# Two transformer blocks on one core: the dense matmuls as one plain float32 matmul each in place of three over rounded parts

## The chip, the cores and the metric

The kernel runs on one core of one Trainium2 chip. The metric is the device time of that core in microseconds, from the first to the last instruction of one launch. Lower is better.

## What is computed

256 tokens of width 1024, in float32, go through two blocks. The reference, cut to what matters:

```python
# first block (c gives shift, scale and gate of both halves: ada = silu(c) @ w_ada + b_ada)
h = modulate(rmsnorm(x, g), sh_m, sc_m)
proj = h @ w_in                       # 1024 -> cq, ckv, k_rope, fq, fk, fv, f_logit, g_mla, g_fox
q  = rmsnorm(cq) @ w_uq;  kv = rmsnorm(ckv) @ w_ukv
y  = sigmoid(g_mla) * (attention(q, k, v) @ w_o_mla) + sigmoid(g_fox) * (attention(fq, fk, fv, log_cum) @ w_o_fox)
x  = x + g_m * (y @ w_out)
h  = modulate(rmsnorm(x, g), sh_f, sc_f)
u  = causal_conv3(h @ w_up)           # 1024 -> 5632
x  = x + g_f * ((silu(gate) * val) @ w_down)
x  = rmsnorm(x)
# second block
proj = rms_norm(x) @ w_in_2           # xc, b_gate, c_gate, q, k, v
h  = x + concat(short_conv(xc, b_gate, c_gate), diff_attention(q, k, v)) @ w_out_2
hn = rms_norm(h)                      # 4 groups of 8 experts, the best 2 of the best group
out = h + sum over the experts e of (silu(hn @ w_gate[e]) * (hn @ w_up[e]) * comb[:, e]) @ w_down[e]
```

## The kernel before

It is one program written by hand for the five engines, ordered by semaphores. There is no scheduler: the order on each engine is the order of the code.

**The dense part.** All dense weights (w_in, w_uq, w_ukv, w_o_mla, w_o_fox, w_out, w_up, w_down, w_in_2, w_out_2, and w_ada for the vector c) are a list of `items` that SyncE (SP) loads one after the other into a ring of three slots of SBUF (line 407). An item of w_in, w_up or w_in_2 is 1024 x 512 float32, 2 MB; `up0` to `up10` are the items of w_up, `dn0` to `dn5` those of w_down, and `q2`, `k2`, `v2`, `xc`, `cg`, `bg`, `w2o_attn` and `w2o_conv` those of the second block. An item is worked off in chunks, of 128 x 1024 weights as a rule.

**The three passes.** A dense product is made of float32r operands, which TensorE reads in reduced precision. Each operand is split in a high part, rounded to float32r, and a low part, the rest. For each chunk, `split` on ScalarE (ACT, line 590) copies the raw weights into `wh` (one of four buffers), and `split` on VectorE (DVE, line 1451) subtracts it from the raw weights into `wl`. The activations are held in two parts as well: `hH` and `hL` (the normed input, by feature), `aH` and `aL` (attention output, latents, the activated FFN), `hnH` and `hnL` (the normed tokens for the experts). Where an activation is produced, ACT writes the high part and DVE then the low one (lines 1477, 1593, 1677, 1723, 1768, 1846, 1963, 1981). `chunk` on TensorE (PE) waits for `chunk_low` and issues for every 128 x 128 block of weights

```python
o_ = ps[:, b0 + m // 2, 256 * (m % 2):256 * (m % 2) + 256]
mm(o_, h[:, cs], xh[:, k, :], st and m % 2 == 0, False)
mm(o_, h[:, cs], xl[:, k, :], False, False)
ins = mm(o_, l[:, cs], xh[:, k, :], False, sp_)
```

where the weights are stationary and the 256 tokens move. For `cq`, `ckv`, `fv`, `uq`, `ukv`, `q2`, `k2` and `v2` it is the other way round (`by_token`): 128 tokens are stationary, and 288 to 512 columns of weights move.

**The order of the dense part** is: projections of the first block; its attention in 16 steps, between which `chunk` puts the gate items g1 to g3; output projections; up and down (items up0 to up5, dn0 to dn2, up6 to up10, dn3 to dn5); norms; q2, k2, v2, xc; the second attention in 8 steps with cg and bg between; the output projection; the router.

**The experts.** All 32 experts are worked off in 8 turns of four, in two pairs (r = 0 and r = 1), for the tokens that chose them (64 places for each expert). `gather` picks the tokens by a product of `hnH` and `hnL` with a matrix of zeros and ones, `pick`, which is float32r too. After it come gate, up, four transposes of the product (line 1410), down, and the product with `putT` that adds the rows to `y_acc`. Gate, up, down and putT are plain float32 matmuls. The gather for the next turn is issued at the end of a turn, and a last one, whose result nobody reads, after the last turn. The 201 MB of expert weights go through eight places of 2 MB: slots 0 to 2 (the ring), 3, 4 and 5 (`work`), 6, and 7 in two halves (`slot7a`, `slot7b`, the latter in `wb`). Slots 6 and 3 and slot7a share memory with `wl`, `wh` and `hL`, so their first loads wait for the last dense chunk. In the loop SP waits for `expert_used` before it loads a place again (lines 475 to 488).

Activations (`Silu`, `Exp`, `Square`) are on ACT, everything else that is elementwise on DVE, and the power of -0.5 of the norms on GpSimd (POOL).

## Time and profile before

| | |
|---|---|
| median of 3 runs | 1144.72 us (1140.96 to 1156.25) |
| profiled execution, its span | 1145.6 us |
| dense part, to the first expert matmul | 643.95 us |
| experts, to the end | 501.7 us |
| busy: PE, its weight loads, DVE, ACT | 90%, 60%, 39%, 34% |
| mean granted TensorE clock | 0.967 |

The profiled execution has no time of its own beside its span; the span stands 0.9 us above the median of the runs. A matmul's busy time overlaps that of the next one, so the time that a stream of matmuls takes is read from the distance of their starts, or from how many there are in a stretch without a gap.

### The profile page before, as it was taken

The numbers are of one execution on the slowest core, as the hardware profiler recorded it, in microseconds if no ns is written. First come the engines' busy times: TensorE is split into PE (matmuls) and PEld (weight loads), VectorE is DVE, ScalarE is ACT, GpSimd is POOL, SyncE is SP. The second block draws the span as 40 slices with busy tenths as digits, with TensorE's granted clock in tenths as the row PEclk, the third lists the DMA queues.
The fourth block names the chain that finished last, engine by engine and source line by source line (L and its number), as shares of the span: only waits on it lengthen the run. The fifth ranks groups of instructions, "written<-read, shape, count | busy, mean of one in ns | idle before, by whom it ended". The sixth has DMA issues, their size and how long they took to land.

```text
span 1145.6 us, 15408 instructions
## 1 busy us (share of the span) xinstructions
PE 1034.9 (90%) x6222; PEld 681.7 (60%) x6222; DVE 444.5 (39%) x829; ACT 388.7 (34%) x675; POOL 23.6 (2%) x50
## 2 busy tenths in 40 slices
PE   3799899999899999979889799999989899798888
PEld 1497767888799999958788434343424224242323
DVE  1543455657578467566664310101111100110111
ACT  0343444554566456445544212030302103020302
POOL 1000000000000000012010000000000000000000
PEclk9799999999899999989889899999989999999999
DMA  9663943284355563625627699999999999999996
GB/s 322 258 220 123 364 184 147 75 285 156 114 181 192 177 199 132 221 89 205 221 88 257 222 379 375 348 387 387 387 387 387 387 387 387 387 387 387 387 387 225
DMA packets 156329, 309.06 MB, mean 270 GB/s; under 512 B 6738, under 2 KB 32376, under 8 KB 153208
## 3 DMA queue, kind: packets, MB, share of 16 engines
q1 hardware_dynamic: 153496, 307.17, 74.0%
q10 hardware_dynamic: 2784, 1.21, 0.4%
q8 instruction: 35, 0.57, 0.2%
q14 instruction: 14, 0.11, 0.0%
HBM read 307.31 MB, written 1.05 MB: 269 GB/s over the span
## 4 chain that ended last, share of the span: by engine, by line
PE 27%; SPq 16%; DMA 5%; DVE 2%; issue 1%; ACT 1%; ACTq 0%; DVEq 0%
PE ps L952 26%; SPq L414 8%; SPq L451 6%; DMA work<-w_exp_down 3%; DMA wb<-w_exp_gate 3%; SPq L418 2%; DVE wc L2080 1%; PE ps L1410 1%; ACT wc L941 0%; PE ps L1332 0%; DVE wb L1896 0%; PE ps L1263 0%; PE ps L1384 0%; DVE wa L1887 0%; DVE wl L1451 0%
## 5 line engine op out<-in xcount | busy, mean ns | idle before, releaser
L1451 DVE TENSOR_TENSOR wl<-ring,wh 128x1024 fp32r<-128x1024 f32 (+4 forms) x156 | 184.1, 1191 | 119.7 <-ACT wh L590 119.3
L590 ACT ACTIVATE wh<-ring 128x1024 fp32r<-128x1024 f32 (+4 forms) x156 | 159.6, 1031 | 149.7 <-PE ps L952 121.8
L952 PE MATMUL ps<-hH,wh 128*128 128x256 f32 x704 | 203.2, 289 | 5.9 <-DVE hL L1477 1.9
L952 PE MATMUL ps<-hH,wl 128*128 128x256 f32 x704 | 199.7, 284 | 0.0
L952 PE MATMUL ps<-hL,wh 128*128 128x256 f32 x704 | 199.7, 284 | 0.0
L952 PE MATMUL ps<-slot,xT 128*64 128x512 f32 x384 | 174.2, 610 | 16.8 <-DMA wb<-w_exp_gate 16.8
L952 PE MATMUL ps<-ring,xT 128*64 128x512 f32 x512 | 168.5, 594 | 1.0 <-DMA slot<-w_exp_up 1.0
L952 PEld LDWEIGHTS ps<-hH,wh 128*128 128x128 f32 x704 | 135.7, 193 | 12.1 <-issue 7.3
L952 PEld LDWEIGHTS ps<-hL,wh 128*128 128x128 f32 x704 | 135.0, 192 | 0.2
L952 PEld LDWEIGHTS ps<-hH,wl 128*128 128x128 f32 x704 | 135.0, 192 | 0.0
L952 PE MATMUL ps<-work,wc 128*64 128x512 f32 x512 | 115.1, 597 | 17.4 <-ACT wc L941 11.0
L952 PEld LDWEIGHTS ps<-ring,xT 128*64 128x64 f32 x512 | 52.5, 137 | 108.4 <-issue 104.8
L2080 DVE TENSOR_TENSOR wc<-wc,ps 128x512 f32<-128x512 f32 x16 | 11.0, 687 | 271.4 <-PE ps L952 271.4
L2093 DVE TENSOR_TENSOR wb<-wb,ps 128x512 f32<-128x512 f32 x64 | 44.0, 687 | 160.3 <-PE ps L952 160.3
L952 PE MATMUL ps<-aH,wh 128*128 128x256 f32 x304 | 86.9, 286 | 2.2 <-DVE aL L1677 1.7
L952 PEld LDWEIGHTS ps<-slot,xT 128*64 128x64 f32 x384 | 53.0, 140 | 59.6 <-issue 38.7
L952 PEld LDWEIGHTS ps<-work,wc 128*64 128x64 f32 x512 | 34.6, 137 | 87.7 <-issue 58.9
L952 PE MATMUL ps<-aL,wh 128*128 128x256 f32 x304 | 86.1, 283 | 0.0
L952 PE MATMUL ps<-aH,wl 128*128 128x256 f32 x304 | 86.1, 283 | 0.0
L952 PE MATMUL ps<-wa 128*128 128x512 f32 (+2 forms) x160 | 71.7, 570 | 0.9 <-ACT work L710 0.9
L952 PEld LDWEIGHTS ps<-aH,wh 128*128 128x128 f32 x304 | 58.4, 192 | 3.0 <-DVE aL L1677 1.9
L952 PEld LDWEIGHTS ps<-aL,wh 128*128 128x128 f32 x304 | 58.1, 191 | 0.0
(310 smaller groups left out, 1240.7 us busy)
## 6 DMA issues: line engine op xcount, KB each, us to landing
work<-w_exp_down SPq DMA_DIRECT2D x64, 1024.0 KB, 14.3
ring<-w_exp_up SPq DMA_DIRECT2D x32, 1024.0 KB, 14.2
ring<-w_exp_gate SPq DMA_DIRECT2D x32, 1024.0 KB, 14.1
slot<-w_exp_up SPq DMA_DIRECT2D x32, 1024.0 KB, 14.2
ring<-w_ada SPq DMA_DIRECT2D x12, 2048.0 KB, 9.1
ring<-w_in SPq DMA_DIRECT2D x12, 2048.0 KB, 8.5
ring<-w_up SPq DMA_DIRECT2D x22, 1024.0 KB, 7.3
slot<-w_exp_gate SPq DMA_DIRECT2D x8, 2048.0 KB, 17.0
```

What stands on the lines that cost most here:

```text
L414: sp.dma_start(slot(i)[:, k0 * width:(k0 + kn) * width].rearrange("p (k n) -> p k n", k=kn), src[:, k0:k0 + kn, :])\
L418: sp.dma_start(dst.rearrange("p (k n) -> p k n", k=4), expert(w_gate, e)[:, k0:k0 + 4, :])\
L451: sp.dma_start(to, expert(w_downx, e + j)[:, :, cs]).then_inc(S(f"downs_half{half}"), 16)
L590: nc.scalar.activation(wh[:, c % CHUNKS, 0:n], src, ACT.Copy).then_inc(S("chunk_high"), 1)
L952: return nc.tensor.matmul(o_, l, r, start=start, stop=stop, skip_group_check=True)
L1410: ins = nc.tensor.transpose(ps[:, 2, f * P:f * P + P], eact[:, f * P:f * P + P], ident[:])
L1451: V.tensor_tensor(wl[:, c % CHUNKS, 0:n], src, wh[:, c % CHUNKS, 0:n].bitcast(F32), ALU.subtract)\
L2080: V.tensor_tensor(eact, sg, ps[:, 1, :], ALU.mult).then_inc(S("e_act"), 1)
L2093: V.tensor_tensor(v, v, ps[:, 6 + i % 2, :], ALU.add).then_inc(S("y_sum"), 1)
```

## The change

Each dense product is one plain float32 matmul: `chunk` reads the raw weights from the ring slot and the activations from one tensor (`hT`, `aT`, `hn_tok`), with a third of the calls. Both `split` functions go, with every step that writes a low part; what wrote the high part now writes the operand (where DVE made a float32 tensor first, it writes the operand itself). `gather` has one product where there were two, and `pick` is float32. The dense ring has five slots, 0, 1, 2, 3 and 6, and an item is waited for by PE at its first chunk; SP waits for `chunk_used` (PE is done with the item) where it waited for `chunk_low` (the item is split). slot7a is memory of its own, and its first load stands ahead of the others.

```diff
 SLOT = 8 * 520
-RING1 = 3
-CHUNK = 2 * 520
-CHUNKS = 4
+RING_SLOTS = (0, 1, 2, 3, 6)
...
+        ring = sb("ring", [P, len(RING_SLOTS), SLOT])
         work = sb("work", [P, 2 * SLOT])
-
-        with nc.sbuf_tensor("wl", [P, CHUNKS, CHUNK], F32R) as wl:
-            pass
-        slot6 = sb("slot6", [P, SLOT])
-        with nc.sbuf_tensor("wh", [P, CHUNKS, CHUNK], F32R) as wh:
-            pass
-        slot3 = sb("slot3", [P, SLOT])
-        with nc.sbuf_tensor("hL", [P, KD, SEQ], F32R) as hL:
-            pass
         slot7a = sb("slot7a", [P, KD * SEQ])
-        hH = sb("hH", [P, KD, SEQ], F32R)
-        aH = sb("aH", [P, 12, SEQ], F32R)
-        aL = sb("aL", [P, 12, SEQ], F32R)
+        hT = sb("hT", [P, KD, SEQ])
...
         for i, it in enumerate(items):
-            it["slot"] = i % RING1
+            it["slot"] = RING_SLOTS[i % len(RING_SLOTS)]
...
-                if i == RING1:
+                if i == 3:
                     load_rows()
-                if i >= RING1:
-                    before = items[i - RING1]
+                if i >= len(RING_SLOTS):
+                    before = items[i - len(RING_SLOTS)]
                     if before["chunks"]:
-                        sp.wait_ge(S("chunk_low"), before["c1"])
+                        sp.wait_ge(S("chunk_used"), before["c1"])
                     else:
...
-            for i in sorted(last, key=lambda i: last[i]["c1"]):
-                sp.wait_ge(S("chunk_low"), last[i]["c1"])
+            final = {it["slot"]: it["c1"] for it in items}
+            in_order = sorted(final, key=lambda i: final[i])
+            for i in in_order:
+                if i == in_order[-2]:
+                    sp.wait_ge(S("att_logits"), 2 * HEADS + 2 * N_HEADS2)
+                    load_half7(slot7b, 3, 4)
+                sp.wait_ge(S("chunk_used"), final[i])
                 if i < 2:
                     for half in range(2):
                         load_gate_half(i, i, half)
+                elif i < 4:
+                    load_up(i - 2, i - 2)
                 else:
-                    load_up(0, 0)
-            sp.wait_ge(S("att_logits"), 2 * HEADS + 2 * N_HEADS2)
-            load_half7(slot7b, 3, 4)
-            sp.wait_ge(S("chunk_used"), n_chunk)
-            load_up(1, 1)
-            load(6, expert(w_gate, 2), 0, KD, D_EXP, "slot6_loaded")
-            load_half7(slot7a[:], 3, 0)
+                    load(6, expert(w_gate, 2), 0, KD, D_EXP, "slot6_loaded")
...
 
-            def split(name, a=0, b=None):
-
-                it = IT[name]
-                for ci in range(a, len(it["chunks"]) if b is None else b):
-                    c = it["c0"] + ci
-                    if ci == 0:
-                        act.wait_ge(S(f"slot{it['slot']}_loaded"), it["loaded"])
-                    if c >= CHUNKS:
-                        act.wait_ge(S("chunk_used"), c - CHUNKS + 1)
-                    src, n = raw_chunk(it, ci)
-                    nc.scalar.activation(wh[:, c % CHUNKS, 0:n], src, ACT.Copy).then_inc(S("chunk_high"), 1)
...
-                        ins = nc.scalar.activation(hH[:, k, :], n_t[:, k, :], ACT.Identity, bias=shift[:, k:k + 1])
-                    ins.then_inc(S("norm_high"), 1)
+                    nc.scalar.activation(hT[:, k, :], n_t[:, k, :], ACT.Identity, bias=shift[:, k:k + 1])\
+                        .then_inc(S("norm_in"), 1)
 
...
@@ -951,47 +833,37 @@
             def mm(o_, l, r, start, stop):
                 return nc.tensor.matmul(o_, l, r, start=start, stop=stop, skip_group_check=True)
 
-            def chunk(name, ci, xh, xl, by_token, banks=None, first=True, last=True, ready=None):
+            def chunk(name, ci, x, by_token, banks=None, first=True, final=True, ready=None):
 
                 it = IT[name]
                 n = it["n"]
                 b0 = it["acc"] if banks is None else banks
                 main = n if n > 520 else min(n, 512)
                 k0, kn = it["chunks"][ci]
-                c = it["c0"] + ci
-                pe.wait_ge(S("chunk_low"), c + 1)
-                for kk in range(kn):
-                    k = k0 + kk
+                if ci == 0:
+                    pe.wait_ge(S(f"slot{it['slot']}_loaded"), it["loaded"])
+                w = slot_view(it)
+                for k in range(k0, k0 + kn):
                     if ready is not None:
                         pe.wait_ge(S(ready[0]), ready[1][k])
-                    st, sp_ = first and k == 0, last and k == it["kn"] - 1
-                    h = wh[:, c % CHUNKS, kk * n:(kk + 1) * n]
-                    l = wl[:, c % CHUNKS, kk * n:(kk + 1) * n]
+                    st, sp_ = first and k == 0, final and k == it["kn"] - 1
                     if by_token:
                         for tt in range(TT):
                             ts = slice(tt * P, tt * P + P)
-                            o_ = ps[:, b0 + tt, 0:main]
-                            mm(o_, xh[:, k, ts], h[:, 0:main], st, False)
-                            mm(o_, xl[:, k, ts], h[:, 0:main], False, False)
-                            ins = mm(o_, xh[:, k, ts], l[:, 0:main], False, sp_)
+                            ins = mm(ps[:, b0 + tt, 0:main], x[:, k, ts], w[:, k, 0:main], st, sp_)
                             if n > main:
-                                o_ = ps[:, 4, tt * (n - main):(tt + 1) * (n - main)]
-                                mm(o_, xh[:, k, ts], h[:, main:n], st and tt == 0, False)
-                                mm(o_, xl[:, k, ts], h[:, main:n], False, False)
-                                ins = mm(o_, xh[:, k, ts], l[:, main:n], False, sp_)
+                                ins = mm(ps[:, 4, tt * (n - main):(tt + 1) * (n - main)], x[:, k, ts], w[:, k, main:n],
+                                         st and tt == 0, sp_)
                     else:
                         for m in range(n // P):
-                            cs = slice(m * P, m * P + P)
-                            o_ = ps[:, b0 + m // 2, 256 * (m % 2):256 * (m % 2) + 256]
-                            mm(o_, h[:, cs], xh[:, k, :], st and m % 2 == 0, False)
-                            mm(o_, h[:, cs], xl[:, k, :], False, False)
-                            ins = mm(o_, l[:, cs], xh[:, k, :], False, sp_)
+                            ins = mm(ps[:, b0 + m // 2, 256 * (m % 2):256 * (m % 2) + 256], w[:, k, m * P:m * P + P], x[:, k, :],
+                                     st and m % 2 == 0, sp_)
                 ins.then_inc(S("chunk_used"), 1)
 
...
+                        pe.wait_ge(S("hn_high"), i + 2)
                     for kk in range(2):
                         k = 2 * i + kk
                         o_ = ps[:, 6 + i % 2, 256 * kk:256 * kk + 256]
                         for tt in range(TT):
-                            mm(o_, hnH[:, tt, k * P:k * P + P], pick[:, tt, :], kk == 0 and tt == 0, False)
-                            ins = mm(o_, hnL[:, tt, k * P:k * P + P], pick[:, tt, :], False, tt == TT - 1)
+                            ins = mm(o_, hn_tok[:, tt, k * P:k * P + P], pick[:, tt, :], kk == 0 and tt == 0, tt == TT - 1)
                     ins.then_inc(S("gathered"), 1)
...
 
-            def split(name, a=0, b=None):
-
-                it = IT[name]
-                for ci in range(a, len(it["chunks"]) if b is None else b):
-                    c = it["c0"] + ci
-                    dve.wait_ge(S("chunk_high"), c + 1)
-                    src, n = raw_chunk(it, ci)
-                    V.tensor_tensor(wl[:, c % CHUNKS, 0:n], src, wh[:, c % CHUNKS, 0:n].bitcast(F32), ALU.subtract)\
-                        .then_inc(S("chunk_low"), 1)
...
                 for k in range(KD):
-                    V.scalar_tensor_tensor(out=n_t[:, k, :], in0=xT[:, k, :], scalar=scale[:, k:k + 1], in1=bc,
-                                           op0=ALU.mult, op1=ALU.mult).then_inc(S("norm_t"), 1)
-                    if k >= 2:
-                        low(k - 2)
-                low(KD - 2)
-                low(KD - 1)
+                    out_, sem = (n_t, "norm_t") if shifted else (hT, "norm_in")
+                    V.scalar_tensor_tensor(out=out_[:, k, :], in0=xT[:, k, :], scalar=scale[:, k:k + 1], in1=bc,
+                                           op0=ALU.mult, op1=ALU.mult).then_inc(S(sem), 1)
 
...
-            split("dn5")
-            split("q2", 0, 2)
             done("dn5")
             for m in range(KD):
                 residual(m, ps[:, 4 + m // 2, 256 * (m % 2):256 * (m % 2) + 256], adaT[:, G_F + m:G_F + m + 1], "xT_ready")
 
 
             cols = norm_mean(2, 3, 2)
-            split("q2", 2, 3)
             dve.wait_ge(S("norm_rstd"), 3)```

**PE, in one of the first block's attention steps** (ident and wc at line 1145: the turn of a head's probabilities; wa and nFT: the scores of the head two steps on). Before:

```order
L952 MATMUL ps<-hH,wh 128x256
L952 MATMUL ps<-hL,wh 128x256
L952 MATMUL ps<-hH,wl 128x256
L1145 MATMUL ps<-ident,wc 128x128 x3
L952 MATMUL ps<-wa 128x128
L952 MATMUL ps<-nFT,ident 128x128
```

The first three rows stand eight times in a row. After, the same step:

```order
L834 MATMUL ps<-hT,ring 128x256 x8
L1017 MATMUL ps<-ident,wc 128x128 x3
L834 MATMUL ps<-wc,wa 64x256
L834 MATMUL ps<-wc,wa 64x128
L834 MATMUL ps<-wa 128x128
L834 MATMUL ps<-nFT,ident 128x128
```

The 24 calls of a chunk are 8, and nothing else on PE is moved.

**DVE, at the second norm of the first block** (L1482 writes `n_t`, which ACT turns into hH; L1477 writes hL). Before:

```order
L1464 COPY wc<-ps 1x256
L1458 TENSOR_SCALAR ms<-ps 128x2
L1451 TENSOR_TENSOR wl<-ring,wh 128x1024
L1482 SCALAR_TENSOR_TENSOR wb<-xT,scale_f,ps 128x256 x3
L1477 SCALAR_TENSOR_TENSOR hL<-wb,adaT,hH 128x256
```

After:

```order
L1325 COPY wc<-ps 1x256
L1319 TENSOR_SCALAR ms<-ps 128x2
L1335 SCALAR_TENSOR_TENSOR wb<-xT,scale_f,ps 128x256 x8
L1561 SCALAR_TENSOR_TENSOR work<-ps,colT,work 128x255 x4
L1561 SCALAR_TENSOR_TENSOR work<-ps,colT,work 128x254 x4
```

The first part that PE can use came behind three steps of DVE, one of ACT and a fourth of DVE; now it comes behind one of DVE and one of ACT.

**SP, at the end of the dense part.** Before:

```order
L451 DMA work<-w_exp_down 128x4x512 [waits k2_turned]
L451 DMA work<-w_exp_down 128x4x512 x3
L414 DMA ring<-w_exp_up 128x4x512 [waits chunk_low]
L414 DMA ring<-w_exp_up 128x4x512
L414 DMA ring<-w_exp_gate 128x4x512 [waits chunk_low]
L414 DMA ring<-w_exp_gate 128x4x512
L414 DMA ring<-w_exp_gate 128x4x512 [waits chunk_low]
L414 DMA ring<-w_exp_gate 128x4x512
L418 DMA wb<-w_exp_gate 128x4x512 [waits att_logits]
L414 DMA slot<-w_exp_up 128x4x512 [waits chunk_used]
L414 DMA slot<-w_exp_up 128x4x512
L414 DMA slot<-w_exp_gate 128x8x512
```

After:

```order
L391 DMA slot7a<-w_exp_gate 128x4x512
L424 DMA work<-w_exp_down 128x4x512 [waits k2_turned]
L424 DMA work<-w_exp_down 128x4x512 x3
L387 DMA ring<-w_exp_gate 128x4x512 [waits chunk_used]
L387 DMA ring<-w_exp_gate 128x4x512
L387 DMA ring<-w_exp_up 128x4x512 [waits chunk_used]
L387 DMA ring<-w_exp_up 128x4x512
L387 DMA ring<-w_exp_up 128x4x512 [waits chunk_used]
L387 DMA ring<-w_exp_up 128x4x512
L391 DMA wb<-w_exp_gate 128x4x512 [waits att_logits]
L387 DMA ring<-w_exp_gate 128x8x512 [waits chunk_used]
L387 DMA ring<-w_exp_gate 128x4x512 [waits chunk_used]
```

Five places (3, 6 and 7a among them) no longer wait together for the last chunk of all: only one of the ring's slots does.

## Rows read from the trace of the kernel before

**Rows 1.** The page: busy time and count by engine; granted clock and GB/s in 40 slices.
```profile
PE 1034.9 (90%) x6222; PEld 681.7 (60%) x6222; DVE 444.5 (39%) x829; ACT 388.7 (34%) x675; POOL 23.6 (2%) x50
...
PEclk9799999999899999989889899999989999999999
...
GB/s 322 258 220 123 364 184 147 75 285 156 114 181 192 177 199 132 221 89 205 221 88 257 222 379 375 348 387 387 387 387 387 387 387 387 387 387 387 387 387 225
```

**Rows 2.** Busy time (and records) by engine in three stretches, with clock and GB/s.
```profile
300.00:330.00 30.00, 30.00 (x256) 30.00 (x255) 21.70 (x31) 17.91 (x24) 0.00 (x0) 1.00 0.44 141
503.00:530.00 27.00, 27.00 (x118) 21.95 (x117) 18.97 (x25) 11.83 (x13) 3.81 (x1) 1.00 0.42 142
698.00:702.00 4.00, 4.00 (x33) 3.82 (x33) 0.59 (x1) 2.48 (x6) 0.00 (x0) 1.00 1.05 387
```

**Rows 3.** PE's groups by shape: stationary size, moving form, records | busy, mean ns | idle before.
```profile
L952 PE MATMUL ps<-hH,wh 128*128 128x256 f32 x704 | 203.2, 289 | 5.9 <-DVE hL L1477 1.9 <-ACT wb L682 1.4 <-DVE wl L1451 1.1
...
L952 PE MATMUL ps<-aH,wh 128*128 128x256 f32 x304 | 86.9, 286 | 2.2 <-DVE aL L1677 1.7 <-issue 0.6
...
L952 PE MATMUL ps<-wa 128*128 128x512 f32 x128 | 62.2, 618 | 0.0
L952 PE MATMUL ps<-hH,aH 128*128 128x256 f32 x144 | 38.6, 304 | 1.5 <-DVE hH L2031 1.5
...
L952 PE MATMUL ps<-wh,hH 128*128 128x512 f32 x64 | 27.4, 428 | 1.8 <-DVE hL L1475 1.8
```

**Rows 4.** PE's timeline: start, length, engine, line, matmul, count; five stretches.
```profile
713.68 0.59 PE L952 MATMUL ps<-ring,xT 128*64 128x512 f32 x1
...
714.11 0.59 PE L952 MATMUL ps<-ring,xT 128*64 128x512 f32 x1
...
284.70 3.61 PE L952 MATMUL ps<-wb,tri_ones 128*1 128x256 f32 x16
...
192.28 0.92 PE L952 MATMUL ps<-work 96*128 96x128 f32 x4
...
152.03 0.70 PE L952 MATMUL ps<-wa 64*128 64x256 f32 x2
...
152.66 0.52 PE L952 MATMUL ps<-nFT,ident 8*128 8x256 f32 x1
```

**Rows 5.** What PE waited for: us in total, times, longest; whole span.
```profile
PE ps L952 <- DMA wb<-w_exp_gate: 16.8, 5, 3.4
...
PE ps L952 <- DVE hL L1477: 4.2, 2, 2.3
...
PE ps L1263 <- DVE wa L1841: 3.2, 2, 2.1
PE ps L952 <- DVE wl L1451: 2.7, 2, 1.5
PE ps L952 <- DVE wb L1865: 2.6, 1, 2.6
PE ps L952 <- DVE hL L1475: 1.8, 1, 1.8
```

**Rows 6.** PE's timeline: the transposes of four pairs of experts.
```profile
658.69 0.66 PE L1410 MATMUL ps<-ident,wc 128*128 128x128 f32 x4 [0.79 <-DVE wc L2080]
...
717.22 0.66 PE L1410 MATMUL ps<-ident,wc 128*128 128x128 f32 x4 [0.79 <-DVE wc L2080]
...
964.45 0.66 PE L1410 MATMUL ps<-ident,wc 128*128 128x128 f32 x4 [0.79 <-DVE wc L2080]
...
1028.88 0.66 PE L1410 MATMUL ps<-ident,wc 128*128 128x128 f32 x4 [0.79 <-DVE wc L2080]
```

**Rows 7.** SP's queue, a stretch of the loop's start.
```profile
702.41 2.65 SPq L451 DMA_DIRECT2D work<-w_exp_down  x1
716.64 0.39 SPq L414 DMA_DIRECT2D ring<-w_exp_up  x1
```

**Rows 8.** PE's timeline: the first record of the last gather.
```profile
1140.20 0.39 PE L952 MATMUL ps<-hH,aH 128*128 128x256 f32 x1
```

More of the change, by code:

```diff
@@ L9 @@
 F32 = mybir.dt.float32
-F32R = mybir.dt.float32r
 I32 = mybir.dt.int32
@@ L162, in slot @@
         def slot(i):
-            if i < RING1:
-                return ring[:, i, :]
-            return {3: slot3[:], 4: work[:, 0:SLOT], 5: work[:, SLOT:2 * SLOT], 6: slot6[:]}[i]
+            if i in RING_SLOTS:
+                return ring[:, RING_SLOTS.index(i), :]
+            return {4: work[:, 0:SLOT], 5: work[:, SLOT:2 * SLOT]}[i]
         rows = wc[:, 0:3 * P].rearrange("p (i n) -> p i n", i=3)
@@ L451, in load_downs @@
                         sp.dma_start(to, expert(w_downx, e + j)[:, :, cs]).then_inc(S(f"downs_half{half}"), 16)
+            load_half7(slot7a[:], 3, 0)
             sp.wait_ge(S("k2_turned"), 2)
             load_downs(0)
-            last = {it["slot"]: it for it in items}
-            for i in sorted(last, key=lambda i: last[i]["c1"]):
-                sp.wait_ge(S("chunk_low"), last[i]["c1"])
+            final = {it["slot"]: it["c1"] for it in items}
[5 more added lines that the diff above has]
+                sp.wait_ge(S("chunk_used"), final[i])
                 if i < 2:
@@ L752, in _ @@
                     nc.scalar.activation(v, v, ACT.Sigmoid).then_inc(S("sig_ready"), 1)
-            split("wo0", 0, 2)
-            for m in range(KD):
-                if m == 4:
-                    split("wo0", 2)
-                act.wait_ge(S("y_ready"), m // 2 + 1)
-                nc.scalar.activation(hH[:, m, :], yF[:, m, :], ACT.Copy).then_inc(S("y_high"), 1)
-            split("wo1")
-            split("up0", 0, 3)
             norm_squares(1)
-            split("up0", 3)
-            norm_high(1, adaT[:, SH_F:SH_F + KD])
+            norm_shift(1, adaT[:, SH_F:SH_F + KD])
             def conv_first(j):
@@ L1063, in _ @@
             ada_turn(0)
-            linear("cq", hH, hL, True, ready=("norm_in", [IN_BASE[0] + k + 1 for k in range(KD)]))
-            linear("ckv", hH, hL, True)
+            linear("cq", hT, True, ready=("norm_in", [IN_BASE[0] + k + 1 for k in range(KD)]))
+            linear("ckv", hT, True)
             pe.wait_ge(S("lat_copied"), 2)
-            linear("fq", hH, hL, False)
+            linear("fq", hT, False)
             pe.wait_ge(S("ada_row"), 1)
@@ L1108, in _ @@
                     ada_turn(1)
-                chunk("g0", ci, hH, hL, False)
+                chunk("g0", ci, hT, False)
             pe.wait_ge(S("rope_done"), 1)
@@ L1174, in _ @@
                         pe.wait_ge(S("gate_out"), 2 * (i // 4) + 2)
-                    chunk(f"g{1 + i // 4}", i % 4, hH, hL, False)
+                    chunk(f"g{1 + i // 4}", i % 4, hT, False)
                 turn(a)
@@ L1287, in _ @@
                 if st < 4:
-                    chunk("cg", st, hH, hL, False)
+                    chunk("cg", st, hT, False)
                 else:
@@ L1291, in _ @@
                         pe.wait_ge(S("cg_out"), 2)
-                    chunk("bg", st - 4, hH, hL, False)
+                    chunk("bg", st - 4, hT, False)
                 if st % 2:
@@ L1302, in _ @@
             pe.wait_ge(S("cy_ready"), 2)
-            o_in = ("mix_low", [1, 2, 3, 4])
-            chunk("w2o_attn", 0, aH[:, 4:8], aL[:, 4:8], False, 0, True, False, o_in)
+            o_in = ("mix_high", [1, 2, 3, 4])
+            chunk("w2o_attn", 0, aT[:, 4:8], False, 0, True, False, o_in)
             pe.wait_ge(S("cv_sq"), 1)
@@ L1323, in _ @@
             ins.then_inc(S("cv_bc"), 1)
[L1324 to L1325 removed]
+            chunk("w2o_attn", 3, aT[:, 4:8], False, 0, True, False, o_in)
+            linear("w2o_conv", aT, False, 0, False, True, ("mixF", [1, 2, 3, 4]))
             for i in range(4):
@@ L1393, in _ @@
                             elif part == 0:
-                                pe.wait_ge(S("slot6_loaded"), turn * 16 + 16)
+                                pe.wait_ge(S("slot6_loaded"), turn * 16 + (base_loaded[6] + 16))
                                 pe.wait_ge(S("slot7_loaded"), turn * 32 + 32)
@@ L2013, in _ @@
             V.tensor_tensor(gtmp, gl, wide(gmax, GROUPS), ALU.subtract).then_inc(S("g_shift"), 1)
-            for i in range(2):
-                low_tokens(i)
             dve.wait_ge(S("places"), 1)
@@ L2045, in _ @@
             pick_tokens(0, 0)
-            for i in range(2, 4):
-                low_tokens(i)
             link(V.tensor_scalar(npass[0:1, 1:2], npass_f[0:1, 0:1], float(CAP - 1), None, ALU.add))
```

291 lines of the change are left out of this document (54 added, 237 removed).

## The prediction

> **What bounds the kernel now.** I first read the page [rows 1]: PE is busy for 90% of the span, DVE and ACT for 39% and 34%, and the memory moves 387 GB/s without a dip in the last third, far below that before. So there are two parts with different limits, and each is read for itself.
>
> In the dense part (643.95 us) the question is whether PE or the splitting on ACT and DVE sets the pace. The windows answer it [rows 2]: from 300 to 330 us there are 256 records of 256 columns in 30.00 us without idle time, 117 ns for each, 118 with a chunk's own edges. From 503 to 530 us records of 512 columns come at 27.00/118 = 229 ns. ACT and DVE are idle for a third of that time and more. A column thus costs PE some 0.45 ns whatever the others do, and the splits are ahead. What PE waited for in this part [rows 5] is 1 to 4 us at single places, most of it behind a step that writes a low part. The dense part is bound by PE's stream of columns.
>
> In the experts' part (501.7 us) PE is near the limit too. The transposes of turn after turn start 717.22 - 658.69 = 58.53 us apart at first, and 1028.88 - 964.45 = 64.43 us late in the loop [rows 6]. A turn loads 25.2 MB, which takes 65.0 us at 387 GB/s [rows 1]. So PE sets the first turns and the memory the later ones; PE's wait for slot7b, 16.8 us in five times of up to 3.4 [rows 5], is that limit seen from PE.
>
> **What a plain float32 matmul costs.** The groups by shape [rows 3] count 128 records for the products with putT, of which the program has 64 (8 turns, 2 pairs, 4 products): a plain matmul is two records, one for each half of its stationary operand. The timeline [rows 4] gives the length of one: gate and up records of 512 columns on the same columns of the array start 714.11 - 713.68 = 0.43 us apart, and the 16 records of 256 columns of a norm's sum take 3.61 us to the end of the last, whose own length is about 0.38: 15 distances of 0.215 us. Four records of 128, 128, 256 and 256 columns on 96 rows end 0.92 us after they start, with no more than the two streams in it. So a record costs 0.215 us at 256 columns and 0.43 at 512, twice a float32r record, and the matmul has two of them: 0.43 and 0.86 us. Three float32r records are 3 x 0.118 = 0.354 and 3 x 0.230 = 0.690 us. **The change takes a third of the calls away and makes each product dearer on the engine that bounds the part.** The trace has no plain matmul with 128 x 128 weights and 256 moving columns; 0.215 a record is the row nearest in columns. From below it is the stream alone, 0.427/2 = 0.213; from above it is the scores on half the rows, where two records take 152.66 - 152.03 = 0.63 us, 0.32 each, since the weights' load is not hidden there [rows 4]. I take 0.216, as the products with putT and the 96-row scores have full or nearly full weights and show no such gap.
>
> The Trainium skill (FP8 and Floating Point Precision, "TensorE Precision Notes") has true FP32 at "4 passes through PE array". At four times a 256-column stream the matmul is an estimate of 0.43 us; the 0.215 us of a record with two records to a matmul agree.
>
> **The change part by part.**
> 1. *Blocks with 256 moving tokens.* 704 + 304 = 1008 [rows 3], each 0.432 - 0.354 = 0.078 us dearer: **+78.6 us**. Nothing hides it: PE has no idle time in those stretches.
> 2. *Token-major products with 512 columns.* 64 [rows 3] and 8 of ukv: 72 x (0.86 - 0.69) = **+12.0 us**.
> 3. *Token-major products with 384, 288 and 8 columns* (28, 16 and 16 in the code). In proportion to columns the first two add about 0.12 and 0.09 us each; the last, two short records for three, gives some back. I take **+3 us**, bounds 0 and +6.
> 4. *Gather.* A gather is 32 float32r records at 4.00/33 = 0.121 us [rows 2], 3.9 us; it becomes 32 records of 0.216, 6.9 us: +3.1 us each time. The first lies ahead of the experts: **+3.1 us**. Those of turns 1 to 7 lie in a PE turn of 58.5 us, which becomes 61.6, still under the memory's 65.0: hidden, as long as the memory stays the limit, and the cover is 3.4 us a turn. Ahead of that limit one is not hidden: SP's loads of the next ups wait until 716.64 us for PE, when the queue has run dry behind the loads of 702.41 [rows 7]. They come 3.1 us later, and all the stream after them: **+3.1 us**. The last gather starts at 1140.20 [rows 8], behind everything, and ends the program: **+2.8 us**.
> 5. *Splits and low parts.* 156 splits each on ACT and DVE go. They hide behind PE's stream today and bring nothing there. They bring something where PE waited for them [rows 5]: the two waits for `wl` go whole (2.7); the three at a norm's end shorten from four steps of DVE and one of ACT to one or two steps in all (3.3 of 6.0); the attention's ends, where DVE had splits before the step that PE waited for, give about 3.5 of 5.8; and half a microsecond comes from the low part of the last head. **-10 us**, bounds -5 and -15 (all of these rows).
> 6. *The ring of five.* PE waited for no dense weights, so deeper prefetch brings nothing. At the end of the dense part the expert places are filled earlier, but they were full before too: PE waits for none of them in the first turns. **0**, bounds 0 and -3. The loads at the start stand in the same order up to the rows of small vectors; two more come right behind these and could hold up nothing that PE awaits but those rows: 0 to +1.
>
> Short stretches at 1.2 GHz (the lower digits of the clock, [rows 1]) follow the waits at the norms. They are counted in time, not in matmuls, and stay as they are.
>
> Sum: 78.6 + 12.0 + 3 + 3.1 + 3.1 + 2.8 - 10 = **+92.6 us**. From the span that is 1145.6 + 92.6 = 1238.2; from the median of the runs, 0.9 lower, **1237 us**.
>
> **The rivals.**
> - *The plain matmul streams once (faster).* If one record of 256 columns at 0.215 did a whole product, the 1008 blocks would save 0.139 us each, 140 us, and with the token-major ones and the waits the time would be near 980. The point from which this side decides is 0.354/2 = 0.177 us a record (0.172 with what the waits give back). For it: the code calls one matmul. Against it: two records for every plain call, and 0.215 each. 2%.
> - *The splits are the limit, and PE only looks busy.* Then taking them away gains more than the matmuls cost. Its place would be the up and down items; ACT at 17.91 and DVE at 21.70 of 30 us, with PE without a gap [rows 2], speak against it. No change at best, 1145. 2%.
> - *The weights' load comes into the open.* At 0.32 us a record [rows 4] the blocks cost 0.64 instead of 0.432, 210 us more: about 1450. The 96-row scores speak against it. 3%. The Trainium skill says it as a rule (TensorE: Matmul & The Clock Gate, "What overlaps and what doesn't"): a weight load overlaps a running matmul only when the row groups differ. By that rule the dense stream, always on the same 128 rows, would pay each load. The 117 ns of the float32r stream, on the same rows throughout, do not agree with it.
> - *The gathers are not hidden.* If PE stays the limit in all turns, because the loads wait for PE more often than I read, seven more gathers count: up to +18 us, 1255. PE's own turn of 61.6 us is near 65.0, which speaks for some of it. 10%.
> - *More of the waits go than I took*, and the experts' loads gain: 1222 to 1230. 10%.
>
> **How the numbers follow.** The forecast holds with 73%: 1237, itself good to some 9 us (4 ns on a record's price alone are 8 us over 2016 records). Bounds of the small terms and the last two rivals widen it to 1218 to 1258. Faster by over 2% (the first rival) 2%, within 2% 2%, slower by over 2% 96%; 2% is about what a measurement of this kernel can tell from no change.
>
> **What would show it.** In the changed kernel, groups with 1408 + 608 records for the blocks and 288 for the gather; some 139 records in a window of 30 us of the up items, against 256; no idle PE there. The first expert matmul at 644 + 87 = 731 us. The transposes of turns 0 and 1 some 61.6 us apart and those of the late turns 65, with PE's wait for slot7b near nothing. DVE and ACT some 200 us less busy each. Wrong would I be if records of the blocks came closer than 0.21 us or farther apart than 0.23, or if the late turns took more than 66 us.

## The result and the profile after

The changed kernel takes 1230.08 us (median of four runs, 1229.28 to 1230.53) against 1147.17 (four runs, 1140.96 to 1156.25): 1.0712 times as long, 95% interval 1.0663 to 1.0762. The forecast was 1237, range 1218 to 1258. The profiled executions span 1228.0 us and, before, 1145.6.

The page of the changed kernel, busy time and count by engine, clock and GB/s in 40 slices:

```profile
PE 1140.7 (93%) x5082; PEld 696.7 (57%) x5082; DVE 239.5 (20%) x611; ACT 221.7 (18%) x488; POOL 19.1 (2%) x50
...
PEclk9899979999999999999999989999999999999999
...
GB/s 329 153 356 105 361 136 104 69 231 214 111 164 137 138 160 149 137 192 82 171 274 104 137 125 387 311 379 387 387 387 387 387 387 387 387 387 387 387 387 204
```

PE has 1140 records fewer than in [rows 1] and 106 us more to do. DVE and ACT have lost 205 and 167 us of work, nearly all of which lay beside PE's stream.

PE's groups by shape:

```profile
L834 PE MATMUL ps<-hT,ring 128*128 128x256 f32 x1408 | 312.0, 382 | 2.3 <-ACT hT L582 1.3 <-DVE wb L1689 1.0
...
L834 PE MATMUL ps<-aT,ring 128*128 128x256 f32 x608 | 134.6, 383 | 1.3 <-issue 0.8 <-ACT aT L672 0.5
...
L834 PE MATMUL ps<-hT,aT 128*128 128x256 f32 x288 | 67.2, 393 | 1.5 <-DVE hT L1773 1.5
```

1408 + 608 records for 1008 blocks: two to each product, as forecast, where [rows 3] had three. Here is a window of the up items, with busy time (and records) of PE, PEld, DVE, ACT and POOL, then granted clock, DMA share, GB/s:

```profile
330.00:360.00 30.00, 30.00 (x140) 26.41 (x140) 7.99 (x18) 6.41 (x11) 0.00 (x0) 1.00 0.41 140
```

30.00/140 = 0.214 us a record, without a gap, against 256 records in [rows 2]. A stretch with nothing else in it prices the block: the 96 blocks of dn0 to dn2 take 41.44 us (401.49 to 442.93), 0.432 each; in the kernel before they take 34.12 (364.68 to 398.80), 0.355.

PE's timeline: the first expert matmul, the transposes of the first two turns and of the last three, the last gather:

```profile
721.09 2.37 PE L834 MATMUL ps<-ring,xT 128*64 128x512 f32 x10
...
735.84 0.65 PE L1281 MATMUL ps<-ident,wc 128*128 128x128 f32 x4 [0.79 <-DVE wc L1820]
...
797.22 0.66 PE L1281 MATMUL ps<-ident,wc 128*128 128x128 f32 x4 [0.79 <-DVE wc L1820]
...
1046.17 0.66 PE L1281 MATMUL ps<-ident,wc 128*128 128x128 f32 x4 [0.79 <-DVE wc L1820]
1111.22 0.66 PE L1281 MATMUL ps<-ident,wc 128*128 128x128 f32 x4 [0.79 <-DVE wc L1820]
1176.28 0.66 PE L1281 MATMUL ps<-ident,wc 128*128 128x128 f32 x4 [0.79 <-DVE wc L1820]
...
1219.71 7.17 PE L834 MATMUL ps<-hT,aT 128*128 128x256 f32 x32
```

The dense part ends at 721.09, 77.1 us later than before (86.7 were forecast). The experts take 1228.0 - 721.09 = 506.9 us, 5.3 more (5.9 were forecast). Turns start 61.38 us apart at first and 65.05 late, as forecast from [rows 6]. From span to span the change costs 82.4 us where the sum in the prediction was 92.6, and the miss of some 10 us lies in the dense part.

What PE waited for: us in total, times, longest:

```profile
PE ps L834 <- DMA work<-w_exp_down: 6.2, 4, 2.1
PE ps L834 <- DMA wb<-w_exp_gate: 5.5, 4, 1.5
...
PE ps L834 <- POOL rstd L524: 3.1, 3, 1.0
PE ps L834 <- ACT hT L582: 2.9, 2, 1.6
...
PE ps L834 <- ACT wb L733: 1.0, 1, 1.0
...
PE ps L834 <- DVE r L1588: 0.8, 1, 0.8
...
PE ps L834 <- DVE hT L1335: 0.7, 1, 0.7
```

The waits for `hL` (4.2 and 1.8 in [rows 5]) have become 2.9 and 0.7, those for `wl` are gone, 2.6 before the second attention is 1.0. The wait for slot7b fell from 16.8 to 5.5, and gave back nothing by itself: the memory was the limit there.

### The profile page after: what moved, and what is told of

Its sections match the earlier page's. It is cut to its first block, busy times and chain, and to the rows that moved or that the text cites. A ratio compares the mean times of both kernels' runs of the same rounds, so it can differ in the third digit from the quotient of the medians.

```text
span 1228.0 us, 12648 instructions
## 1 busy us (share of the span) xinstructions
PE 1140.7 (93%) x5082; PEld 696.7 (57%) x5082; DVE 239.5 (20%) x611; ACT 221.7 (18%) x488; POOL 19.1 (2%) x50
## 3 DMA queue, kind: packets, MB, share of 16 engines
HBM read 307.31 MB, written 1.05 MB: 251 GB/s over the span
## 4 chain that ended last, share of the span: by engine, by line
PE 73%; SPq 21%; DVE 2%; DMA 2%; issue 1%; ACT 1%; POOL 0%; ACTq 0%; DVEq 0%
PE ps L834 71%; SPq L387 10%; SPq L424 7%; SPq L391 3%; SPq L349 1%; DMA work<-w_exp_down 1%; DMA wc<-lambda_k 0%; DVE wc L1820 0%; PE ps L1017 0%; PE ps L1281 0%; ACT wc L823 0%; PE ps L993 0%; PE ps L1204 0%; POOL rstd L524 0%; PE ps L1255 0%
## 5 line engine op out<-in xcount | busy, mean ns | idle before, releaser
L834 PE MATMUL ps<-hT,ring 128*128 128x256 f32 x1408 | 312.0, 382 | 2.3 <-ACT hT L582 1.3
L834 PEld LDWEIGHTS ps<-hT,ring 128*128 128x128 f32 x1408 | 267.7, 191 | 44.2 <-issue 6.6
L834 PE MATMUL ps<-ring,xT 128*64 128x512 f32 x896 | 224.1, 594 | 6.8 <-DMA wb<-w_exp_gate 5.5
L834 PEld LDWEIGHTS ps<-ring,xT 128*64 128x64 f32 x896 | 70.9, 137 | 152.8 <-issue 139.2
L834 PE MATMUL ps<-aT,ring 128*128 128x256 f32 x608 | 134.6, 383 | 1.3 <-issue 0.8
L834 PE MATMUL ps<-work,wc 128*64 128x512 f32 x512 | 114.3, 596 | 17.2 <-ACT wc L823 11.0
L834 PEld LDWEIGHTS ps<-aT,ring 128*128 128x128 f32 x608 | 116.2, 192 | 17.8 <-issue 1.2
L834 PEld LDWEIGHTS ps<-work,wc 128*64 128x64 f32 x512 | 35.0, 137 | 86.2 <-issue 61.3
L834 PE MATMUL ps<-ring,hT 128*128 128x512 f32 (+2 forms) x224 | 80.4, 519 | 2.3 <-ACT hT L582 1.6
L834 PE MATMUL ps<-wa 128*128 128x512 f32 (+2 forms) x160 | 72.8, 578 | 0.9 <-ACT work L653 0.9
L834 PE MATMUL ps<-hT,aT 128*128 128x256 f32 x288 | 67.2, 393 | 1.5 <-DVE hT L1773 1.5
L1820 DVE TENSOR_TENSOR wc<-wc,ps 128x512 f32<-128x512 f32 x16 | 11.0, 688 | 279.6 <-PE ps L834 279.6
L1561 DVE SCALAR_TENSOR_TENSOR work<-ps,colT,work 128x255 f32<-128x255 f32 (+1 forms) x88 | 36.3, 475 | 146.7 <-ACT work L701 146.3
L834 PEld LDWEIGHTS ps<-ring,hT 128*128 128x128 f32 x224 | 41.4, 197 | 41.2 <-issue 35.2
L834 PEld LDWEIGHTS ps<-hT,aT 128*128 128x128 f32 x288 | 55.8, 196 | 15.4 <-DVE wb L1833 6.0
L834 PEld LDWEIGHTS ps<-wa 128*128 128x128 f32 (+1 forms) x160 | 25.5, 191 | 47.4 <-issue 25.6
L826 ACT ACTIVATE wa<-ps 128x512 f32<-128x512 f32 x32 | 19.1, 598 | 112.6 <-PE ps L834 112.6
L834 PE MATMUL ps<-ring,cact 128*1 128x512 f32 x192 | 26.4, 682 | 10.9 <-ACT cact L586 10.9
```

The costliest lines, as they stand in the source:

```text
L826: nc.scalar.activation(eout[:, 512 * hf:512 * hf + 512], ps[:, 3 + hf, :], ACT.Copy)\
L834: return nc.tensor.matmul(o_, l, r, start=start, stop=stop, skip_group_check=True)
L1561: ins = V.scalar_tensor_tensor(out=v, in0=src, scalar=colT[:, ROW[row] + tile:ROW[row] + tile + 1], in1=v, op0=ALU.mult, op1=ALU.add)
L1820: V.tensor_tensor(eact, sg, ps[:, 1, :], ALU.mult).then_inc(S("e_act"), 1)
```

## The experiments

Three questions: are the forecast's terms right one by one, where did 10 us more relief come from, and is there a version that beats both kernels. The kernel before was timed again with each group: medians of 1153.38 (first four kernels), 1149.28 (next four) and 1148.32 (last three). It scatters by 15 us, the changed kernel by 1; so plain versions are best compared with 1230.08, and the stages of the profiled runs with each other. The changed kernel was not timed again, while the median of the one before moved by 5 us from group to group; a difference of plain versions counts only where the spans of the profiled runs show it too.

Two sums over the dense part are used below. One is all that PE waited: 61.6 us before, 49.4 in the changed kernel. The other is what slow clock costs. At 1.2 GHz plain records of 256 columns start 0.427 us apart where they start 0.216 apart at 2.4 GHz (splits_beside, 323 to 327 us), float32r records 0.213 where they start 0.118 apart (the kernel before, 294 to 301 us). So of PE's busy time in the stretches with a granted clock of 0.5, half is lost, or 45% for float32r records. By this estimate it is 23.2 us before and 18.5 in the changed kernel.

**1. plain_with_splits.** `chunk` of the kernel before reads the raw slot:

```diff
-    mm(o_, h[:, cs], xh[:, k, :], st and m % 2 == 0, False)
-    mm(o_, h[:, cs], xl[:, k, :], False, False)
-    ins = mm(o_, l[:, cs], xh[:, k, :], False, sp_)
+    ins = mm(ps[:, b0 + m // 2, 256 * (m % 2):256 * (m % 2) + 256], h[:, m * P:m * P + P],
+             xh[:, k, :].bitcast(F32), st and m % 2 == 0, sp_)
 # h is slot_view(it)[:, k, :]; the same for by_token. SP:
-    sp.wait_ge(S("chunk_low"), before["c1"])
+    sp.wait_ge(S("chunk_used"), before["c1"])
```

> The kernel before with one thing changed: each dense product is one plain float32 matmul that reads the raw weights in the ring and the high part of the activations (the low parts of both are made and waited for, but not used, so the sum lacks them). Every split, every wait for a low part, the ring of three and the gather with two products stay. Theory (the forecast's +78.6, +12 and +3 for the matmuls are right, and what was missing, some 10 us more relief than taken, comes from the splits' absence): 1147 + 94 = 1241 us, good to 4. Rival (the plain matmuls cost less than the forecast says, and the splits' absence gave the 10 us that were forecast): 1231.

Measured: 1266.55 us (1259.31 to 1267.8), ratio 1.0971 (1.0914 to 1.1028). Above both, so it decides between neither. The experiment had a second change in it that I had priced at nothing: a slot is held until PE is done with it. Runs 2, 3 and 4 take the two apart.

**2. ring_of_three.** The changed kernel with the dense items in three slots:

```diff
+DENSE = (0, 1, 2)
-    it["slot"] = RING_SLOTS[i % len(RING_SLOTS)]
+    it["slot"] = DENSE[i % len(DENSE)]
 # and the experts' first loads in the order of the kernel before
```

> The changed kernel with the dense items in slots 0, 1 and 2 alone; slots 3 and 6 stay empty until the loads of the experts, which stand in the order of the kernel before. Theory (PE waits for no dense weights, deeper prefetch brings nothing): 1230 to 1231. Rival (the ring of five is where the unforeseen 10 us come from): 1236 to 1240, with waits of PE for the ring's loads in the dense part.

Measured: 1240.66 us (1239.10 to 1243.45), 10.6 more than the changed kernel. Its first expert matmul starts at 732.72, 11.6 later, and PE has a wait that the changed kernel hasn't:

```profile
PE ps L835 <- DMA ring<-w_in: 8.0, 2, 5.5
```

5.5 us before ckv and 2.5 before g0. PE waits 8.3 us more in the dense part, and slow clock costs 2.8 more, 11.1 of the 11.6 together. The theory of the ring falls for the changed kernel, and the rival (1236 to 1240) holds: with three slots it takes 10.6 us more.

**3. late_release.** The kernel before with that wait of SP alone:

```diff
-    sp.wait_ge(S("chunk_low"), before["c1"])
+    sp.wait_ge(S("chunk_used"), before["c1"])
 # the same ahead of the experts' first loads
```

> The kernel before, with SP waiting until PE is done with a slot's last chunk (as the changed kernel does) before it loads the slot again, where it waited for the split alone. Nothing else is changed. Theory (a ring of three that is held longer lets PE run out of weights; that is why ring_of_three lost 10 us and why the ring of five is worth something in the changed kernel): slower than before by 8 to 20 us, with waits of PE for low parts of weights that hang on a load. Rival (the three slots suffice in the kernel before in either case): no change.

Measured: 1182.93 us (1179.08 to 1184.78), ratio 1.0294 (1.0238 to 1.0351): some 34 us, all in the dense part, and more than the bound that I gave. PE's waits:

```profile
PE ps L952 <- DVE wl L1451: 12.8, 5, 7.2
...
PE ps L1145 <- DVE wc L1672: 7.0, 2, 5.2
```

The first was 2.7 [rows 5]. A slot freed when its last chunk is split is free up to four chunks before PE is done with it; in the kernel before, this is what made three slots enough. All waits in the dense part grow by 23.6 us, from 61.6 to 85.2. The rest is slow clock, which costs 33.8 us where it cost 23.2; PE runs at 1.2 GHz through most of these 16 us:

```profile
172.00:188.00 16.00, 16.00 (x63) 9.62 (x62) 6.32 (x19) 3.48 (x11) 0.00 (x0) 0.57 0.40 133
```

**4. splits_beside.** The clean form of run 1: five slots, and the splits' results in small scratch places.

```diff
+    wl = sb("wl", [P, CHUNK], BF16)
+    wh = sb("wh", [P, 2, CHUNK], BF16)
-    nc.scalar.activation(wh[:, c % CHUNKS, 0:n], src, ACT.Copy)
+    nc.scalar.activation(wh[:, c % 2, 0:n], src, ACT.Copy)
-    V.tensor_tensor(wl[:, c % CHUNKS, 0:n], src, wh[:, c % CHUNKS, 0:n].bitcast(F32), ALU.subtract)
+    V.tensor_tensor(wl[:, 0:n], src, src, ALU.subtract)
```

> The changed kernel's matmuls, gather and ring of five slots, with all the work of the splits put back beside them: ACT copies every chunk and DVE subtracts on every chunk, at the places in the program and with the waits of the kernel before, and the low parts of the activations are made and waited for. Their results go to small scratch places (bfloat16, the same number of elements) and are not used, so the sum lacks the low parts. Theory (the ring of three that was held until PE was done spoiled the run plain_with_splits, and the splits' absence gave all of the dense part's relief, 19.6 us): 1250 us, good to 4. Rival (of the relief only the norms' 5 us and some 5 at the attention are the splits', the rest comes from the plain stream itself, behind which more can hide): 1240. Rival (the late slots were innocent, splits beside plain matmuls cost what plain_with_splits shows): 1262 and more.

Measured: 1245.13 us (1243.68 to 1245.98), 15.0 above the changed kernel, half way between the theory (1250, good to 4) and the first rival (1240); the first expert matmul at 735.33, 14.2 later. The up items show that the splits themselves cost nothing beside the stream, as many records in 30 us as without them:

```profile
335.00:365.00 30.00, 30.00 (x141) 26.41 (x140) 19.39 (x29) 16.94 (x22) 0.00 (x0) 1.00 0.41 140
```

What they cost is waits at a stage's edge, and these are the rows of before again, but for `wl` (2.7 there):

```profile
PE ps L956 <- POOL rstd L552: 4.9, 3, 2.0
...
PE ps L956 <- DVE hL L1474: 4.2, 2, 2.3
...
PE ps L956 <- DVE wb L1862: 2.6, 1, 2.6
PE ps L956 <- DVE wl L1448: 2.1, 2, 1.5
PE ps L956 <- DVE hL L1472: 1.8, 1, 1.8
PE ps L956 <- DVE r L1803: 1.8, 1, 1.8
PE ps L956 <- DVE aL L1674: 1.7, 1, 1.7
```

Against the changed kernel's rows (3.1; 2.9; 1.0; none; 0.7; 0.8; 0.5) that is 19.1 - 9.0 = 10.1 us of waits, of 10.8 in all. Slow clock makes up most of the rest of the 14.2: it costs 22.0 us in this run and 18.5 in the changed kernel, 3.5 more.

**5. norm_chains.** The changed kernel with the old chains in the three norms alone:

```diff
+    def low(k):
+        dve.wait_ge(S("norm_high"), IN_BASE[n] + k + 1)
+        V.tensor_tensor(junk[:, k, :], xT[:, k, :], hT[:, k, :], ALU.subtract).then_inc(S("norm_in"), 1)
```

> The changed kernel with the steps put back that stood in the three norms' chains before: DVE writes a stand-in for the low part behind each normed piece, two pieces late, and PE waits for it; a DVE step as long as a split stands at the three places where a split stood in the second and third norm. Nothing else is changed. Theory (the unforeseen relief is shorter waits at the norms and the stretches at 1.2 GHz behind them, which come back with the waits): PE's waits there grow by some 5 us, a granted clock of 0.5 is seen again behind the second norm, the third or both, and the time is 1238, 8 us more. First rival (waits alone, the clock does not follow them): 1235. Second rival (the relief lies elsewhere, as at the attention's ends): 1230 to 1232.

Measured: 1235.99 us (1234.96 to 1236.95), 5.9 more, the first rival. The first expert matmul starts 4.9 us later, and PE's waits there grew by 5.0: 5.8 for `junk`, 4.9 for `rstd`, 1.8 for `r`, against 3.6, 3.1 and 0.8. (A wait for a small load at another place is 1.6 us shorter.) Slow clock did come back at the norms, as the theory had it (at 315 to 318 us, and at 554 to 564 where the changed kernel has 556 to 559), but it went elsewhere: in the dense part it costs 18.8 us against 18.5.

**6. two_product_gather.** The changed kernel with the old gather:

```diff
-    ins = mm(o_, hn_tok[:, tt, k * P:k * P + P], pick[:, tt, :], kk == 0 and tt == 0, tt == TT - 1)
+    mm(o_, hnH[:, tt, k * P:k * P + P], pick[:, tt, :], kk == 0 and tt == 0, False)
+    ins = mm(o_, hnL[:, tt, k * P:k * P + P], pick[:, tt, :], False, tt == TT - 1)
```

> The changed kernel with the gather as it was before: high and low part of the normed tokens, two float32r products with 256 columns, and DVE's four steps that write the low part. Theory (terms of part 4: first gather 3.1, the stall of SP's queue 3.1, last gather 2.8, all others hidden under the memory): 1221 us, 9 less; the transposes of the first turns 58.3 us apart, the late ones 65. Rival (no stall follows from it, only the first and the last gather count): 1224. Rival (gathers are not hidden, all nine count): 1202.

Measured: 1220.32 us (1219.94 to 1221.11), 9.8 less, as in the theory (1221). The dense part (with the first gather) gives 4.5, the experts 5.5. Turns start 58.5 us apart at first and 65.06 late, and the memory shows as PE's wait again:

```profile
PE ps L838 <- DMA wb<-w_exp_gate: 16.7, 5, 3.4
```

**7. two_passes.** The kernel before with two of its three products:

```diff
-    mm(o_, h[:, cs], xl[:, k, :], False, False)
```

> The kernel before without the product of the weights' high part with the activations' low part (two float32r products for each block where there were three, the splits and low parts still made and waited for; the sum lacks that part). Theory (PE's stream sets the dense part): 1008 x 0.118 + 72 x 0.230 + 3 = 138 us less in the dense part, if the splits keep pace; DVE had 21.7 us of work in 30 of PE's, which are now 20, so in the up items it is the next limit and keeps 10 to 20 us of it: 1020 to 1030 us. Rival (the splits are the limit already): no change.

Measured: 1051.09 us (1045.18 to 1061.43), ratio 0.9116 (0.9055 to 0.9177). The rival falls: with a third of PE's stream gone 98 us go, so PE was the limit. But 138 were there to gain, and the theory's 1020 to 1030 is missed too. The up items show a cause, with DVE near full and PE with gaps:

```profile
300.00:330.00 30.00, 25.57 (x212) 25.00 (x211) 28.27 (x46) 22.15 (x33) 0.00 (x0) 1.00 0.57 212
```

In 30 us there are 106 products here and 85 in [rows 2]; two records of 0.117 us would have made 128. So the splits' limit is less than one pass away from the three-pass kernel. Over the whole dense part PE waits 95.4 us where it waited 61.6, and slow clock costs 33.6 where it cost 23.2; these two are 44 us, about the 40 that are missing.

**8. trimmed.** The kernel before with shorter waits and no last gather:

```diff
-    if k >= 2:
-        low(k - 2)
+    if k >= 1:
+        low(k - 1)
 # split("up0", 3) and split("q2", 2..3) behind or inside norm_apply, not ahead of it
 with pe.Fori(0, TURNS) as g:
+    gather(turn)
     ...
-    gather(turn + 1)
```

> The kernel before, three passes and all, with shorter waits: at the norms DVE writes a low part one piece late, not two, and the splits that stood inside the second and third norm's chain come behind it or in its middle; the gather stands at a turn's start, not at its end, so that the last one, which nobody reads, goes. Theory (waits at the norms are worth what PE waits there, and stretches at 1.2 GHz are not tied to them): 4 us at the norms and 2 at the end, 6 less than before. Rival (the clock follows the waits): 10 to 12 less. Rival (what is gained at a norm is waited for behind it, as the moved splits come late): 2 less, the end alone.

Measured over ten runs: 1141.48 us (1136.95 to 1153.27), ratio 0.9951 (0.9912 to 0.999). Of the profiled run's 10.0 us less, 7.5 are in the dense part and 2.5 at the end. The waits for `rstd` and `r` fell by 1.8 and 0.9 as meant; that for `hL` did not (4.3), since DVE waits for ACT there, not for its own second piece. All waits in the dense part are 2.0 us less (59.6), and slow clock costs 4.1 us less (19.1).

**9 to 11. filled, trimmed_filled, plain_filled.** PE works on nothing while it waits:

```diff
+    def fill(bank, count):
+        for _ in range(count):
+            mm(ps[:, bank, 0:P], ident[:], ident[:], True, True)
-    norm_spread("norm_rstd", 2, rstd, 5)
+    norm_spread("norm_rstd", 2, rstd, 5, 0, (2, 8))   # fill(2, 8) ahead of its wait
+    fill(2, 8)
     # up0 follows; the same at six more places
```

> The kernel before, with PE kept busy in eight of its waits: plain 128 x 128 products of the identity with itself into a bank of PSUM that is free there, 5 to 20 calls, each some 0.22 us, so many that they end just before the wait does (before cq, at the second and third norm, before the second attention, before the turn of its outputs, at the router and before the first gather). They change no result. Read in the kernel before, the stretches at 1.2 GHz behind these places add up to some 20 us of (1 - granted clock) x time in the dense part. Theory (PE's clock falls where PE stood idle shortly before, so those stretches go): 8 to 16 us less than before, and the granted clock stays at 1 from 292 to 300 and from 494 to 502 us. Rival (the clock falls whatever PE did, or the fillers count as nothing): no change, or 1 to 3 us more where a filler ends late.

> The kernel trimmed (three passes, shorter waits at the norms, no last gather) with the same fillers, shorter where its waits are shorter. Theory (the clock follows PE's idle time): another 6 to 12 us less than trimmed, some 1132, which would be faster than before by 1.5%. Rival (the clock is not to be had that way): as trimmed.

> The changed kernel with the gather of two float32r products (as in two_product_gather) and the same fillers, cut to its own waits. Its stretches at 1.2 GHz behind such places are fewer; the two that cost most are at 550 to 557 and 700 to 715 us. Theory: 4 to 8 us less than two_product_gather's 1220. Rival: as two_product_gather.

Measured: filled 1141.52 us (1136.14 to 1145.62, ten runs), ratio 0.9942 (0.9906 to 0.9977), just short of the theory's 8 to 16; trimmed_filled 1133.53 (1131.05 to 1141.84, eleven runs), ratio 0.9905 (0.987 to 0.994), 8.0 less than trimmed as in the theory, and faster than both kernels, if by 1% only; plain_filled 1214.79 (1208.89 to 1217.02), 5.5 less than two_product_gather (theory 4 to 8). Windows behind the second and the third norm, of the kernel before:

```profile
292.00:302.00 10.00, 8.34 (x47) 8.37 (x48) 7.47 (x17) 4.90 (x9) 0.00 (x0) 0.66 0.63 207
494.00:504.00 10.00, 8.04 (x26) 6.39 (x27) 8.77 (x25) 4.35 (x9) 0.00 (x0) 0.66 0.60 211
```

and of filled:

```profile
292.00:302.00 10.00, 9.88 (x84) 9.57 (x83) 8.10 (x18) 5.13 (x10) 1.04 (x1) 1.00 0.64 210
494.00:504.00 10.00, 9.78 (x44) 7.88 (x44) 10.00 (x27) 5.47 (x10) 0.00 (x0) 1.00 0.45 173
```

The clock stays at 2.4 GHz, and up0 to up5 take 67.8 us where they took 71.0. Over the dense part slow clock costs 15.1 us, 8.1 less than before, and the dense part is 5.9 shorter. At the router it failed. There the clock fell at 616.8 us, ahead of the fillers, while PE was busy with transposes and the router's records of 36 columns; these took 6.7 us where they take 3.7 before, the fillers began at half speed and ended 1 us late, and the stage cost 4.4 us more:

```profile
612.00:632.00 20.00, 19.14 (x118) 17.75 (x117) 9.23 (x41) 7.21 (x18) 0.70 (x1) 0.74 0.85 316
```

## Why the prediction was right, point by point

- *PE's stream of columns bounds the dense part.* Right; two_passes shows it, and how near the next limit is.
- *Two records a product at 0.216 us (parts 1 and 2).* Right: 0.432 a block from dn0 to dn2. The same stretch of before gives 0.355 for three records, so a block costs 0.076 more, 77 us in all. The prediction says that each record is one half of the stationary operand; the rows show two records and two loads of weights for each product (PEld has 5082 records as PE has), and not what each carries. Before to splits_beside, with the splits' waits in both, the dense part grows by 91.4 us where the terms (78.6, 12.0, 3, and 3.1 of the gather) say 96.7. Stage by stage dn0 to dn5, up6 to up10, the first attention and its output projections agree within 0.3 us. The missing 5 lie in pieces of 1 to 2 us ahead of that attention, at wo, at the first up items, at q2 to v2, at cg and bg and at the gather, with 1.3 the other way at w2o. These are the places where slow clock comes and goes. The sums over the dense part account for 4.3 of them: the blocks' own price is 1.7 less (76.9 for 78.6), slow clock costs 22.0 us in splits_beside and 23.2 before, and PE waits 60.2 and 61.6. This is added up from the traces; no experiment isolates it.
- *The weights' load comes into the open (rival).* Refuted: 0.214 us a record in the up items, always on the same 128 rows. The rule of the Trainium skill (TensorE: Matmul & The Clock Gate, "What overlaps and what doesn't") that a load overlaps only with other row groups does not hold for this stream. The 0.32 us of a record on 64 or 8 rows, which the prediction puts down to a load in the open, were not looked into.
- *The gather (part 4).* 9.0 us forecast, 9.8 measured by two_product_gather; the hidden gathers are hidden, late turns 65.06 us apart in both.
- *Splits and low parts, -10 us (part 5).* The row sum came out, 10.1 us of waits by splits_beside, but by luck: the waits that it named gave 7.3 where it had 10, and two that it did not name gave 2.8 (`rstd` 1.8, `r` 1.0). The term was still too small: the step that failed is "Short stretches at 1.2 GHz ... stay as they are". Splits_beside lost 14.2 us in the dense part, 3.5 of them to slow clock, and filled took 6 us out of the kernel before with nothing but fillers. Nor do the stretches simply follow each wait: norm_chains put 5.0 us of waits back and paid 0.3 for the clock.
- *The ring of five, 0 (part 6).* The number holds against the kernel before, the reason given does not. The change also made SP wait for PE's end of a slot where it had waited for the split, an edit that I left without a price. By itself it costs 34 us in the kernel before; in the changed one, with three slots, it leaves 10.6 to pay, and the two new slots take them away. Two terms that cancel, where I wrote one that is nothing.

Together: of the 9.6 us missed in the dense part, some 4 are relief beyond part 5's sum, most of it slow clock (3.5), and some 5 stand against the terms of parts 1 to 4: a price of the blocks that was 1.7 too high, less waiting (1.4), less slow clock (1.2), and 1 us of unsettled cause. The rest of the forecast stands.

That the number missed by 7 us and not by 10 is luck. The forecast starts from the profiled span less 0.9, since the span stood above the median of three runs. But in each run of the kernel before that has both, the time is 2.1 to 2.5 us above its span (1.9 in the changed kernel). The execution with the span of 1145.6 was thus one of about 1148 us, and the starting point some 3 us too low.

## What to carry to other kernels

A plain float32 matmul is two records, each of twice the length of a float32r record (0.215 against 0.118 us for 256 columns), so three float32r records are cheaper (0.355 against 0.432 us for 128 x 128 x 256) as long as their splits hide; count records, not calls. When an edit changes who frees a buffer, price it alone, even if the same edit adds buffers. Where PE waits 2 us at a stage's edge, look at the granted clock behind the wait too: behind the second norm it cost 3.2 us after waits of 1.9 and 1.9, and work on nothing took it away.

## What the hardware showed that was not expected

- Slow clock follows waits, but not only these. In the changed kernel it stands in the first attention too (159.9 to 173.5 us), with PE without a gap in the window below, behind a stretch of transposes and of scores on 64 and 8 rows. The last gap ahead of it, 0.9 us, ended at 156.8. A chunk in it takes 5.75 us instead of 3.46. It also comes and goes at one place between kernels that are alike there (this stretch is 3.4 us long in norm_chains). That the kernel before scatters by 15 us for this reason is likely and was not shown: among the 22 runs beside the last three kernels, the nine with spans up to 1142.5 us have mean clocks of 0.963 to 0.970, and the three above 1150 have 0.951 to 0.959.

```profile
160.00:174.00 14.00, 14.00 (x41) 6.88 (x41) 4.30 (x16) 1.97 (x8) 0.00 (x0) 0.52 0.45 150
```

- A wait added to a kernel can cost more than itself by near half: late_release has 23.6 us more of PE's waits in the dense part and is 34 us slower there. Slow clock costs 10.6 us more in it (33.8 against 23.2), which with the waits makes 34.2.
